# Low halves of every second operand tile on GpSimd, high halves on VectorE, in both layer norms

## What is computed

```python
def _layer(x, ...):
    ...
    y = gated @ w_out
    alpha = (2.0 * DEPTH) ** 0.25
    return _layer_norm(alpha * x + y, ln_gain, ln_bias)

def second_block(x, ...):
    x = x + FFN_RES * _swiglu(_rmsnorm(x, norm_ffn1[l]), w_ffn1_gu[l], w_ffn1_down[l])
    ...
```

## Time and profile before

| | |
|---|---|
| Median of 3 runs | 3499.53 us (3497.16 to 3499.81) |
| The profiled execution's own time | 3501.15 us |
| Its span in the profile | 3499.4 us |
| TensorE's mean granted clock | 0.992 of full |
| TensorE, VectorE, GpSimd, ScalarE busy | 96%, 44%, 43%, 28% |

### The profile page before, as it was taken

One profiled execution on the slowest core, in us unless ns is written; L12 is line 12 of the kernel. 1 busy time (PEld: TensorE's weight loads), 2 busy tenths in 40 slices (PEclk: granted clock), 3 DMA queues, 4 the chain that ended last, 5 costly groups with the idle time before them and its releaser, 6 DMA issues.

```text
span 3499.4 us, 48575 instructions
## 1 busy us (share of the span) xinstructions
PE 3359.7 (96%) x19508; PEld 1699.9 (49%) x19508; DVE 1544.3 (44%) x2384; ACT 965.9 (28%) x1782; POOL 1514.4 (43%) x986
## 2 busy tenths in 40 slices
PE   7999997999999799999999999999999999999999
PEld 4555653545554344444445544555554444444444
DVE  3364547135546743333112365655565653333100
ACT  1434322233331410000002455555544320000000
POOL 3555652445664233333333465555554423333332
PEclk9999999999999899999999999999999999999999
DMA  3112112112121011111222111111012111111112
GB/s 124 42 48 62 52 58 87 49 38 67 35 81 43 30 49 48 50 52 51 70 68 85 34 51 50 53 51 50 28 57 85 52 37 54 48 51 51 50 50 81
DMA packets 55197, 194.28 MB, mean 56 GB/s; under 512 B 7408, under 2 KB 7792, under 8 KB 54512
## 3 DMA queue, kind: packets, MB, share of 16 engines
q1 hardware_dynamic: 52576, 182.96, 16.7%
q10 hardware_dynamic: 2448, 8.91, 0.6%
HBM read 172.97 MB, written 12.58 MB: 53 GB/s over the span
## 4 chain that ended last, share of the span: by engine, by line
PE 87%; DVE 5%; issue 3%; ACT 3%; POOL 1%; DMA 0%; DVEq 0%; POOLq 0%; ACTq 0%
PE pair L1058 25%; PE pair L1060 24%; PE pair L1059 24%; PE pair L1261 3%; PE pair L1230 2%; PE pair L1242 2%; DVE arena L1889 2%; PE pair L1455 1%; PE pair L1429 1%; PE pair L1440 1%; PE pair L1078 1%; POOL panel_parts L867 1%; PE pair L1383 1%; DVE arena L2383 1%; ACT arena L1803 0%
## 5 line engine op out<-in xcount | busy, mean ns | idle before, releaser
L1058 PE MATMUL pair<-operand,panel_parts 128*128 128x512 f16 x2816 | 1075.3, 382 | 59.8 <-POOL panel_parts L867 25.7
L1059 PE MATMUL pair<-operand,panel_parts 128*128 128x512 bf16 x2816 | 1072.9, 381 | 0.0
L1060 PE MATMUL pair<-operand,panel_parts 128*128 128x512 f16 x2816 | 1072.5, 381 | 0.0
L866 POOL TENSOR_SCALAR panel_parts<-panel_raw 128x1024 f16<-128x1024 f32 (+3 forms) x286 | 292.8, 1024 | 1492.0 <-PE pair L1060 1014.6
L867 POOL TENSOR_TENSOR panel_parts<-panel_raw,panel_parts 128x1024 bf16<-128x1024 f32 (+3 forms) x286 | 652.5, 2281 | 23.8
L1058 PEld LDWEIGHTS pair<-operand,panel_parts 128*128 128x128 f16 x2816 | 276.3, 98 | 416.1 <-issue 119.5
L1058 PE MATMUL pair<-arena,panel_parts 128*128 128x512 f16 (+2 forms) x1200 | 452.7, 377 | 10.9 <-DVE arena L1889 3.1
L1060 PE MATMUL pair<-arena,panel_parts 128*128 128x512 f16 (+2 forms) x1200 | 451.7, 376 | 0.0
L1059 PE MATMUL pair<-arena,panel_parts 128*128 128x512 bf16 (+2 forms) x1200 | 451.6, 376 | 0.0
L900 POOL TENSOR_SCALAR arena<-arena,row_inv 128x256 f32<-128x256 f32 (+7 forms) x256 | 339.4, 1338 | 255.5 <-DVE row_inv L1955 255.5
L1060 PEld LDWEIGHTS pair<-operand,panel_parts 128*128 128x128 bf16 x2816 | 276.7, 98 | 336.2 <-issue 6.6
(11 more groups left out here) (197 smaller groups left out, 3841.8 us busy)
## 6 DMA issues: line engine op xcount, KB each, us to landing
panel_raw<-in_wgu SPq DMA_DIRECT2D x88, 512.0 KB, 3.5
panel_raw<-in_wl SPq DMA_DIRECT2D x58, 512.0 KB, 3.5
panel_raw<-in_wm SPq DMA_DIRECT2D x56, 512.0 KB, 3.6
panel_raw<-in_wdn SPq DMA_DIRECT2D x32, 512.0 KB, 3.5
residual<-residual_spill SPq DMA_DIRECT2D x15, 512.0 KB, 6.2
panel_raw<-in_wl SPq DMA_DIRECT2D x18, 384.0 KB, 3.1
panel_raw<-in_wdn SPq DMA_DIRECT2D x16, 384.0 KB, 3.1
residual<-in_xT ACTq DMA_DIRECT2D x8, 512.0 KB, 11.5
```

The source lines that it names most:

```text
L866: chained(nc.gpsimd.tensor_scalar(hi[:, 0:cols], RAW[:, s, 0:cols], HI_MAX, -HI_MAX, ALU.min, ALU.max))
L1058: nc.tensor.matmul(out, stat[0], mov[0], start=first, stop=False)
L1059: nc.tensor.matmul(out, stat[0], mov[1], start=False, stop=False)
L1060: return nc.tensor.matmul(out, stat[1], mov[0], start=False, stop=last)
```

## The change

In both layer norms the low half of tiles 1, 3, 5 and 7 is made by GpSimd with a new helper `low_parts`. VectorE makes only the high half of these, and counts up `x_split` after it. GpSimd counts up a new semaphore `x_low`. TensorE waits for both before the products of an odd tile, and so does ScalarE before it writes the `GAINED` buffer of an odd tile again. The even tiles are split as before.

```diff
+            def low_parts(l):
+                for k in range(1, KT, 2):
+                    c = slice(k * T, (k + 1) * T)
+                    pool.wait_ge(x_split, 8 * (l + 1) + k + 1)
+                    src = GAINED[k % 2] if l == LAYERS - 1 else tview(XT, k)
+                    nc.gpsimd.tensor_tensor(XL[:, c], src, XH[:, c], ALU.subtract).then_inc(x_low, 1)
...
                 pool.wait_ge(masks_made, l + 2)
+                if l > 0:
+                    low_parts(l - 1)
                 follow((l, -1, 0))
...
                 for j in range(2):
                     panel(f"gu{idx}", 0, j, 1024, None)
+                if idx == 1:
+                    low_parts(LAYERS - 1)
                 for j in range(2, 4):
...
                     pe.wait_ge(x_split, l * 8 + k + 1)
+                    if l > 0 and k % 2:
+                        pe.wait_ge(x_low, 4 * (l - 1) + k // 2 + 1)
...
                     pe.wait_ge(x_split, xbase + k + 1)
+                    if idx == 1 and k % 2:
+                        pe.wait_ge(x_low, 4 * (LAYERS - 1) + k // 2 + 1)
...
                     act.wait_ge(x_split, 8 * LAYERS + 8 * n + k - 1)
+                    if n == 0 and k % 2:
+                        act.wait_ge(x_low, 4 * (LAYERS - 1) + k // 2)
...
                     if k >= 2:
                         if l == LAYERS - 1:
-                            split_gained(0, k - 2)
+                            dve.wait_ge(gained, k - 1)
                         else:
                             dve.wait_ge(affine_done, l * 8 + k)
-                            split_x(k - 2, tview(XT, k - 2))
+                        src = GAINED[k % 2] if l == LAYERS - 1 else tview(XT, k - 2)
+                        if k % 2:
+                            c = slice((k - 2) * T, (k - 1) * T)
+                            V_.tensor_scalar(XH[:, c], src, HI_MAX, -HI_MAX, ALU.min, ALU.max).then_inc(x_split, 1)
+                        else:
+                            split_x(k - 2, src)
```

More of the change, by code:

```diff
@@ L523, in build @@
         x_split = sem("x_split")
+        x_low = sem("x_low")
         rope_c_done = sem("rope_c_done")
@@ L1598, in keep_layer @@
                             act.wait_ge(x_split, 8 * (l + 1))
+                            if l > 0:
+                                act.wait_ge(x_low, 4 * l)
                             if l > 0:
```

## The result

The changed kernel took 3506.74 us in the median of 10 runs (3498.7 to 3511.38), the kernel before 3498.03 in 10 runs (3493.43 to 3500.4). The ratio is 1.0023, with a 95% interval of 1.0012 to 1.0033: slower by 4 to 12 us. The forecast was 3505.0.

What follows compares the result with a forecast made beforehand. The prediction took TensorE to bound the stretch after layer 0 and ScalarE that after layer 1. Losses of 3.4 + 2.1 = 5.5 us on the 3499.53 median gave 3505.0 us, range 3500.5 to 3508.5.

Steps and rivals of the forecast that it cites:

- What bounds the two stretches: TensorE at 2.59 us a tile after layer 0, ScalarE's copies at 3.26 us a tile after layer 1.
- The ceiling: Most that a quicker VectorE could give back: 0 us after layer 0 and 1.7 us after layer 1.
- Exclusion: In both stretches VectorE and GpSimd block each other on a shared port; 2.1 us of GpSimd takes 2.1 from VectorE.
- The order at each meeting: VectorE's next instruction goes ahead of GpSimd's subtraction, which hears of the high half about 0.1 us later.
- The stretch after layer 0: TensorE waits 2.0 and 1.3 us before tiles 3 and 5 and reaches tile 7 3.4 us later.
- VectorE's period: After layer 0, two tiles on VectorE go from 6.00 to 6.96 us, with high halves counted at 0.72.
- The stretch after layer 1: GpSimd's last low half waits for VectorE's first addition of squares, so TensorE starts tile 7 2.1 us later.
- The sum: Losses after layer 0 and layer 1 together: 3.4 + 2.1 = 5.5 us.
- the rival of the clock: New TensorE waits cost one or two stretches of lower clock, 1.7 us each: 3506.7 or 3508.4; chance 0.18.
- No slack behind the stretches: Later waits follow from TensorE's products, so the delay passes on whole; rival that it is lost again: 3501.6, chance 0.06.

Runs made afterwards that it cites:

- no_odd_lows: Changed kernel with the low halves of tiles 1, 3, 5 and 7 made and awaited by nobody in both norms: 3494.59 us, ratio 0.9994.
- squares_last: Kernel before, with ScalarE making the eight squares after all gained copies in the norm of layer 1: 3496.15 us, ratio 0.9995.
- memset_lows: Changed kernel with each GpSimd subtraction replaced by two memsets of the low half: 3499.11 us, ratio 1.0004.
- tile7_back: Changed kernel with the low half of tile 7 back on VectorE in both norms, GpSimd keeping tiles 1, 3 and 5: ratio 1.0021.
- after_again: The changed kernel itself, unaltered, measured once more: 3504.73 us in 12 runs, ratio 1.0021.

## Why the prediction was right or wrong

**What bounds the two stretches** held. TensorE bounds the first (no_odd_lows: next to nothing to gain) and ScalarE the second (squares_last: 2.8 us won by ScalarE's order alone). The ceiling, 0 + 1.7 us, was measured as 0.4 to 0.6 and 1.2. The 0 was a little too low: I took VectorE's margin at tile 7, 1.7 us, and it is 0.24 at tile 5, so that TensorE bounds the first stretch narrowly, and not in every execution.

**Exclusion** held: VectorE's instruction takes 2.62 or 3.03 where it meets GpSimd's, GpSimd's 2.50 to 3.04, and memset_lows gives the cause. The order at each meeting was the one forecast, VectorE's next instruction first: the multiplication at tiles 1 and 3, the clip at tile 5, the addition at tile 7 of the second stretch.

**The stretch after layer 0** was mis-sized: 3.4 forecast, 2.5 measured. The step was VectorE's period. With no wait between the high half and the multiplication, they start 0.60 apart and not 0.72; and GpSimd's subtraction holds VectorE for 1.9 (2.62 - 0.69), not 2.1. Two tiles take 6.67 us and not 6.96, and low half 5 comes 0.8 earlier than worked out. TensorE's waits fell where they were put, before tiles 3 and 5, with 1.3 and 0.8 us for 2.0 and 1.3. In six of the eight profiles with the edit after layer 0 it also waited for low half 1, for 0.3 to 0.6 us. That costs nothing more, since A is the same in all eight (27.86 to 27.87). Against the 25.24 to 25.55 of the unchanged stretch the loss is 2.3 to 2.6.

**The stretch after layer 1**: 2.1 forecast; 1.95 to tile 7 and 1.8 at the panel. tile7_back shows that it is the last low half and nothing else, and memset_lows that less than half of it, 0.84, comes without exclusion.

**The sum**, 5.5, is 4.3 by the distances and 3.5 to 3.9 by the runs' spans without the clock. The difference of the medians came out at 8.7 (3506.74 - 3498.03), and at 6.1 in after_again (3504.73 - 3498.68), since 3 to 4 us more are lost at the lower clock. That has the size of the rival of the clock, to which I gave 0.18, but not its mechanism: I put the loss behind the new waits, where 3 of 8 executions have it, and its true place and cause are open. That 3505.0 lies only 1.7 below the measured 3506.74 is therefore in part luck. The waits were 1.2 too many, the clock was left out of the sum, and the kernel before, taken at 3499.53 from three runs, has 3498.03 in ten. 1.0023 is just beyond 0.2%, to which I gave 0.20, and the likeliest case as I priced it lay within.

**No slack behind the stretches** held. From the product behind the panel after layer 1 to the end it is 2292.7 us before (3499.4 - 1206.7), 2293.3 in after_again and 2292.7 in tile7_back, so nothing of the delay was made up there. Between the two stretches, from the first panel's product to the next tile 0, it is 554.8 before and 551.7 to 556.6 in all the kernels, longer and shorter with the clock; there it is the clock-free spans, 3.5 to 3.9 us longer in the changed kernel, that leave little room for slack.

## What to carry to other kernels

Handing a two-input operation from VectorE to an idle GpSimd does not relieve VectorE if VectorE reads two tiles of SBUF or clips meanwhile; here 2.1 us of GpSimd took 1.9 us from VectorE to save it 1.14. That it pays beside other work of VectorE no run here shows. Ask first which engine sets the pace where the work is done: a kernel with the work left out altogether is a cheap upper bound, and here it was 2 us. And the last piece of a sequence should stay with the faster engine: tile7_back won back all of the 1.8 us after layer 1.

## What was not expected of the hardware

GpSimd's memset, which reads nothing, held up VectorE's clip (1.51 and 1.27 us for 0.69) but not its multiplication (1.22), and a clip held up the memset (1.49 for 0.95). A distance between TensorE's products repeats to 0.02 us from one execution to the next where a wait for VectorE or GpSimd lies within it (A 27.86 to 27.87 in eight profiles), and moves with the rise of the clock where none does, while the same kernel's total varies by up to 13 us (3498.4 to 3511.79 in after_again). Products that started before the clock had risen gave part of their lead back: 0.87 us of lead left 0.3, in one execution of each kernel.
